# Down projection of a hybrid decoder step: the late loads move from GpSimd's queue to SyncE's, and four sums are added to the output later

## The chip, the cores and the metric

The kernel runs on one core of a Trainium2 chip. The metric is the device time of one execution in microseconds (us). The engines of the core are TensorE (PE: matmuls, and PEld for its weight loads), VectorE (DVE), ScalarE (ACT), GpSimd (POOL) and SyncE (SP), which here only issues DMAs and waits. They run their own programs side by side and meet at semaphores. DMAs that SP issues are in a hardware queue (q1 in the profile), those that POOL issues in a software queue (q0); both are served by the same 16 DMA engines.

## The reference

One inference step of a one-layer decoder with 1024 prompt tokens and 32 sample tokens: projection, sparse attention, a state-space mixer, and at the end the feed-forward part. The change touches only the last product of it:

```python
def finish(x, o_att, y_ssd, W):
    mix = jnp.concatenate([o_att..., y_ssd...], axis=-1)
    h = x + mix @ W['w_out']
    u = rmsnorm(h, W['norm_ffn'])
    return h + (jax.nn.silu(u @ W['w_gate']) * (u @ W['w_up'])) @ W['w_down']
```

All is float32; g = silu(u @ w_gate) * (u @ w_up) has 1056 rows (tokens) and 2816 columns, w_down is 2816 x 1024, the result is 1056 x 1024.

## The kernel before, in words

The stages run one after another: projection, prompt attention, state-space mixer, sample attention, output mixing, feed-forward. The last, `stage_ffn`, first makes g in 11 turns over pairs of column blocks (L2911 is its matmul), then does the down projection.

**The product.** The down projection is a fast 2 x 2 matrix multiplication with seven products instead of eight. Tokens are cut into two halves of 512 (32 tokens are left over), the 2816 inner rows into 11 pairs (`PAIRS`) of two 128-row blocks, the 1024 output columns into two halves of 512 (`NC`). `DOWN = (5, 3, 2, 4, 1, 6, 7)` is the order of the products. Each product takes 11 steps, one per pair, so there are 77 steps; step j belongs to group n = j // 11. A step needs a block of g sums (`g_x`, called gd_whole in the profile, 128 x 512, computed in the first part and stored in DRAM as g_sums) and one piece of w_down or the sum of two (`w`, `w_x`).

**float32 by parts.** g and w are each split into a high part, rounded for the matmul, and the low rest. ACT makes the high parts (gd_hi L3201, wd_hi L3196), DVE the sums of w (wd_whole, L3263) and the low parts (gd_lo L3275, wd_lo L3270). TensorE multiplies three combinations (L3244), each 128 rows x 512 columns. A step has four tiles q = 0 to 3 of 128 tokens, so 12 matmuls. In the groups of products 3 and 2 (n = 1 and 2) there are four more matmuls a step (L3254) for the 32 leftover tokens, called rest.

**Buffers.** g has six slots (`G_SLOTS`). SP loads the block of step j when step j - 6 has been used by PE (`s.used`), in `down_sync`. The w parts have ten slots.

**PSUM and drains.** A product gathers its 11 steps in four PSUM tiles, one for each q. Six banks are in turn (`D_BANKS`), so at a group's first step tiles 2 and 3 need the banks of tiles 0 and 1 of the group just before. PE waits for `s.drained` there. `drains(n)` in `down_vector` adds a finished product's tiles to y_sums in SBUF (L3293): two additions a tile for products 5, 3, 2, 4 and 1, one for 6 and 7. y_sums starts as h, which is loaded from DRAM; `drains(0)` waits for its top half (`h_in[0]`, four loads), `drains(1)` for the bottom half. DVE's program is one list: at step j it does the low part of w, that of g, the sum of w for the next step or the one after, and, at one place in each group, the drains of the group before. `D_ADDED_AT` gives that place.

**Loads.** SP loads the first pieces w(1,1) and the first g blocks while the last turn of the first part is still running. All else (rest, h, w(0,1), w(0,0), w(1,0), and the rest rows of h) is issued by POOL in `down_pool` at once, when the first part's matmuls are done and its last stores have landed. POOL has no other work by then.

Of the kernel before, what the change touches and what calls it, by code (L numbers as in the profile page):

```python
# [17 lines left out]
P = 128  # L18
# [15 lines left out]
NS = DB * DS  # L34
# [2625 lines left out]
NC = DM // 2  # L2660
PAIRS = FT // 2
# [3 lines left out]
D_W = {1: ((0, 0), (1, 1), ALU.add), 2: ((0, 0),), 3: ((0, 1), (1, 1), ALU.subtract), 4: ((1, 0), (0, 0), ALU.subtract), 5: ((1, 1),),  # L2665
       6: ((0, 0), (0, 1), ALU.add), 7: ((1, 0), (1, 1), ALU.add)}
D_REST = {3: ((0, 1), (1, 1)), 2: ((0, 0), (1, 0))}
D_ADDED_AT = {3: 2, 2: 3, 4: 3, 1: 3, 6: 3, 7: 3}
D_INTO = {1: ((0, 0, ALU.add), (1, 1, ALU.add)), 2: ((1, 0, ALU.add), (1, 1, ALU.subtract)), 3: ((0, 1, ALU.add), (1, 1, ALU.add)),
          4: ((0, 0, ALU.add), (1, 0, ALU.add)), 5: ((0, 0, ALU.subtract), (0, 1, ALU.add)), 6: ((1, 1, ALU.add),), 7: ((0, 0, ALU.add),)}  # L2670
D_BANKS, D_REST_BANKS = (6, 0, 7, 1, 3, 2), (4, 5)
# [7 lines left out]
def g_block(i, p):  # L2679
    return (i - 1) * PAIRS + p  # L2680
# [28 lines left out]
def stage_ffn(nc, io, m):  # L2709
# [5 lines left out]
    top = Region(nc, m.gate_raw_end, m.end)  # L2715
# [17 lines left out]
    d = place_down(nc, m, m.base_end + 14 * kh * QUARTER * 4, d_low, io)  # L2733
# [23 lines left out]
    with stage(nc, "landed*2 w_sum w_hi w_split u_sum u_sum_pool u_hi u_split m_done copied c_done silu_done g_ready "  # L2757
# [3 lines left out]
        with nc.Block() as block:  # L2761
            @block.sync
            def _(sp):
# [50 lines left out]
                load(slice(0, 1), 1)  # L2814
                over_pairs(sp, turn)
                down_sync(sp, s, d)

            @block.scalar
# [102 lines left out]
            @block.gpsimd  # L2921
            def _(pool):
                for k in range(POOL_SUMS):
                    i, a, b, op = U_SUMS[k]
                    nc.gpsimd.tensor_tensor(m.u_whole[1, i][:, :, :], m.u_whole[1, a][:, :, :], m.u_whole[1, b][:, :, :],
                                            op).then_inc(s.u_sum_pool, 1)
                down_pool(pool, s, d)

            @block.vector
            def _(dve):  # L2930
# [128 lines left out]
def place_down(nc, m, early_end, low_at, io):  # L3059

    early, late = Region(nc, m.base_end, early_end), Region(nc, early_end, m.end)
    g_x, g_lo, g_hi, w_x, w_lo, w_hi = [], [], [], [], [], []
    for name, slots, x, lo, hi in (("g", G_SLOTS, g_x, g_lo, g_hi), ("w", W_SLOTS, w_x, w_lo, w_hi)):
        for k in range(slots):
            region = early if k < D_EARLY else late
            x.append(nc.alloc_sbuf_tensor_at(f"{name}d_whole_{k}", [P, NC], F32, offset=region.at))
            lo.append(region(f"{name}d_lo_{k}", [P, NC], F32R))
            hi.append(region(f"{name}d_hi_{k}", [P, NC], F32R))
    w = {(1, 1): [early(f"w_22_{p}", [P, NC]) for p in range(PAIRS)]}
    w[0, 1] = [late(f"w_12_{p}", [P, NC]) for p in range(PAIRS)]  # L3070
    rest = late("rest_parts", [P, FT, 2 * NS], F32R)
    rest_x = late("rest_whole", [P, FT, NS])
    y = late("y_sums", [P, 2, 4, DM])
    for r in range(2):
        w[r, 0] = [late(f"w_{r + 1}1_{p}", [P, NC]) for p in range(PAIRS)]
    rest_y = late("rest_y", [P, DM])
    rest_low = nc.alloc_sbuf_tensor_at("rest_low", [P, NC], F32, offset=low_at)
    return named(g_x=g_x, g_lo=g_lo, g_hi=g_hi, w_x=w_x, w_lo=w_lo, w_hi=w_hi, w=w, rest=rest, rest_x=rest_x, y=y,
                 rest_y=rest_y, rest_low=rest_low, bank=m.bank, g_dram=m.g_dram, rest_dram=m.rest_dram, h_dram=io.h_dram,
                 wd=io.w_down.rearrange("o (f p) n -> p (o f) n", p=P), yp=io.y_prompt.rearrange("o n c -> (o n) c"),  # L3080
                 ys=io.y_sample.rearrange("b t c -> (b t) c"))


def rest_rows(k):

    return slice(2 * QUARTER * k + NC, 2 * QUARTER * (k + 1))


def w_number(piece, p):
    return (2 * piece[0] + piece[1]) * PAIRS + p  # L3090


def down_load_w(engine, s, d, piece, p):
    r, c = piece
    engine.dma_start(d.w[piece][p][:, :], d.wd[:, 2 * p + r, c * NC:(c + 1) * NC]).then_inc(s.w_in[w_number(piece, p)], 16)


def down_load_g(sp, s, d, j):
    i, p = DOWN[j // PAIRS], j % PAIRS
    sp.dma_start(d.g_x[j % G_SLOTS][:, :], d.g_dram[:, g_block(i, p), :]).then_inc(s.g_in[j % G_SLOTS], 16)  # L3100


def down_first_loads(sp, s, d):
    for j in range(D_EARLY):
        down_load_w(sp, s, d, (1, 1), j)
        down_load_g(sp, s, d, j)
    for p in range(D_EARLY, PAIRS):
        down_load_w(sp, s, d, (1, 1), p)
# [4 lines left out]
        down_load_g(sp, s, d, j)  # L3113


def down_pool(pool, s, d):
    top = [("h", 0, q) for q in range(4)]
    bottom = [("h", 1, q) for q in range(4)]
    w = lambda r, c, p: ("w", (r, c), p)
    later = ["rest"]  # L3120
    for q in range(4):
        later += [top[q], w(0, 1, q)]
    later += [w(0, 1, p) for p in range(4, PAIRS)] + bottom
    later += [w(r, 0, p) for p in range(PAIRS) for r in range(2)] + ["rest_h"]

    def one_of(what):
        if what == "rest":
            pool.wait_ge(s.plain_stored, 32 * PAIRS)
            pool.wait_ge(s.second_stored, 48 * PAIRS)
            pool.wait_ge(s.s5_stored, 16 * PAIRS)  # L3130
            pool.wait_ge(s.first_stored, 48 * PAIRS)
            pool.dma_start(d.rest_x[:, :, :], d.rest_dram[:, :, :]).then_inc(s.rest_in, 16)  # L3132
        elif what == "rest_h":
            for k in range(2):
                pool.dma_start(d.rest_y[k * NS // 2:(k + 1) * NS // 2, :], d.h_dram[rest_rows(k), :]).then_inc(s.rest_h_in, 16)
        elif what[0] == "h":
            r = 2 * QUARTER * what[1] + P * what[2]
            pool.dma_start(d.y[:, what[1], what[2], :], d.h_dram[r:r + P, :]).then_inc(s.h_in[what[1]], 16)
        else:
            down_load_w(pool, s, d, what[1], what[2])  # L3140

    pool.wait_ge(s.m_done, 28 * PAIRS)
    for what in later:
        one_of(what)


def down_sync(sp, s, d):
    def store(a, c, q):
        r, cols = 2 * QUARTER * a + P * q, slice(c * NC, (c + 1) * NC)
        inside = min(P, SEQ - r)  # L3150
        sp.dma_start(d.yp[r:r + inside, cols], d.y[0:inside, a, q, cols]).then_inc(s.y_stored, 16)
        if inside < P:
            sp.dma_start(d.ys[0:P - inside, cols], d.y[inside:P, a, q, cols]).then_inc(s.y_stored, 16)

    def stores(n, a, c):
        for q in range(4):
            sp.wait_ge(s.drained, DRAINED[4 * n + q])
            store(a, c, q)

    for j in range(G_SLOTS, D_STEPS):  # L3160
        sp.wait_ge(s.used, j - G_SLOTS + 1)
        if j == PAIRS - 1:
            sp.wait_ge(s.s5_stored, 16 * PAIRS)
        down_load_g(sp, s, d, j)
        if j == 31:
            stores(1, 0, 1)
        if j == 45:
            sp.wait_ge(s.rest_y, 2)
            sp.dma_start(d.yp[rest_rows(0), :], d.rest_y[0:NS // 2, :]).then_inc(s.y_stored, 16)
            sp.dma_start(d.ys[NS // 2:NS, :], d.rest_y[NS // 2:NS, :]).then_inc(s.y_stored, 16)  # L3170
        if j == 53:
            stores(3, 1, 0)
    stores(5, 1, 1)
    stores(6, 0, 0)
    sp.wait_ge(s.y_stored, 16 * 20)
# [103 lines left out]
def down_vector(nc, dve, s, d, last_token_sums):  # L3279
    def drains(n):  # L3280
        if n < 2:
            dve.wait_ge(s.h_in[n], 16 * 4)
        if n > 0:
            dve.wait_ge(s.drained, DRAINED[4 * n - 1])
        for q in range(4):
            if q < 3:
                dve.wait_ge(s.tile_done, 3 * n + q + 1)  # L3287
            else:
                dve.wait_ge(s.used, PAIRS * (n + 1))
            got = d.bank[D_BANKS[(4 * n + q) % len(D_BANKS)]][:, :]  # L3290
            for a, c, op in D_INTO[DOWN[n]]:
                y = d.y[:, a, q, c * NC:(c + 1) * NC]
                nc.vector.tensor_tensor(y, y, got, op).then_inc(s.drained, 1)  # L3293
# [15 lines left out]
    for j in range(2, D_STEPS):  # L3309
        if j == 4:  # L3310
            last_token_sums()
        if j == 9:
            dve.wait_ge(s.rest_hi, 1)
            nc.vector.tensor_tensor(d.rest[:, :, NS:2 * NS], d.rest_x[:, :, :], d.rest[:, :, 0:NS].bitcast(F32),
                                    ALU.subtract).then_inc(s.rest_split, 1)
        if j > PAIRS and j % PAIRS == D_ADDED_AT[DOWN[j // PAIRS]]:
            drains(j // PAIRS - 1)
# [151 lines left out]
```

## Time and profile before

| | before |
|---|---|
| median of 3 runs | 1769.87 us (1769.34 to 1775.06) |
| profiled execution | 1769.87 us, span 1768.1 us |
| busy: PE, PEld, DVE | 95%, 81%, 65% |
| busy: ACT, POOL | 43%, 24% |
| mean granted TensorE clock | 0.983 of full speed |
| DMA, SP's queue q1 | 121.66 MB |
| DMA, POOL's queue q0 | 80.46 MB |
| down projection, first to last PE start | 1533.7 to 1764.0 us |

The span goes from the first to the last instruction of the program; the time of an execution has a little around it. Busy time of PE is the time in which at least one matmul is under way; matmuls overlap, so a matmul of 0.39 us can start every 0.23 us. An idle time is shown in brackets before the instruction that ends it, with the one that released it. DMA landing times are counted from the issue. A time in the rows below is counted from the start of the span.

### The profile page before, as it was taken

What the parts mean: (1) busy time and instruction counts of PE and PEld (TensorE: products, weight loads), DVE (VectorE), ACT (ScalarE), POOL (GpSimd) and SP (SyncE); (2) the same over time, 40 slices, a digit from 0 to 9 for tenths busy, and PEclk for the clock granted to TensorE, in tenths of its full rate; (3) what the DMA queues carried; (4) which work ended last, traced back from release to release, by engine and by line L of the source; (5) the groups of instructions that cost most, each with busy time, mean ns of one, the idle gap of its engine ahead of it and who ended that gap; (6) DMA issues with size and microseconds to landing.
All of it is one profiled execution on the core that took longest, in us unless ns stands there. A gap on an engine that the chain in (4) does not pass through costs nothing. (4 is left out here: it accounts for less than half of the span.)

```text
span 1768.1 us, 32859 instructions
## 1 busy us (share of the span) xinstructions
PE 1673.0 (95%) x11957; PEld 1427.5 (81%) x11957; DVE 1151.3 (65%) x2521; ACT 764.2 (43%) x1593; POOL 431.9 (24%) x532
## 2 busy tenths in 40 slices
PE   5999999899998989998987996999999999999999
PEld 5999999688877666655655876999999999977887
DVE  6632247765665655556464368977777888687885
ACT  6322453677774235456443233433232233365342
POOL 1421110766664553334352001000000000050000
PEclk9999999899999999999998998999999999999999
DMA  5633211121001247547593232332222233493343
GB/s 157 105 104 107 53 43 26 25 50 24 21 15 25 67 127 283 196 136 273 175 396 135 72 98 63 100 104 90 93 93 90 95 108 102 160 390 97 95 119 107
DMA packets 158855, 204.19 MB, mean 115 GB/s; under 512 B 55110, under 2 KB 109423, under 8 KB 158674
## 3 DMA queue, kind: packets, MB, share of 16 engines
q1 hardware_dynamic: 136058, 121.66, 23.1%
q0 software_dynamic: 22368, 80.46, 12.9%
q8 instruction: 73, 1.20, 0.3%
q10 hardware_dynamic: 312, 0.52, 0.1%
q14 instruction: 44, 0.36, 0.1%
HBM read 164.69 MB, written 37.90 MB: 115 GB/s over the span
## 5 line engine op out<-in xcount | busy, mean ns | idle before, releaser
L2911 PE MATMUL banks<-u_sum,w_sum 128*128 128x264 f32 x3696 | 450.0, 284 | 9.7 <-DVE w_sum L2945 9.7
L2911 PEld LDWEIGHTS banks<-u_sum,w_sum 128*128 128x128 f32 x3696 | 449.7, 189 | 9.9 <-issue 9.8
L470 PE MATMUL banks<-u_parts_mix,w_in_parts 128*128 128x352 f32 x1440 | 244.2, 327 | 4.5 <-DVE u_parts_mix L837 4.5
L470 PEld LDWEIGHTS banks<-u_parts_mix,w_in_parts 128*128 128x128 f32 x1440 | 231.2, 189 | 7.8 <-DVE u_parts_mix L837 4.9
L1979 PE MATMUL banks<-turned,cmp_w 128*128 128x512 f32 x256 | 133.2, 603 | 4.7 <-DVE turned L2106 3.0
L2104 ACT ACTIVATE turned<-banks 128x512 f32<-128x512 f32 (+1 forms) x136 | 78.8, 587 | 125.0 <-PE banks L1967 124.8
L3244 PE MATMUL banks<-wd_hi,gd_hi 128*128 128x512 f32 x308 | 119.9, 389 | 1.0 <-DVE gd_lo L3275 1.0
L3244 PE MATMUL banks<-wd_lo,gd_hi 128*128 128x512 f32 x308 | 120.0, 390 | 0.0
L3244 PE MATMUL banks<-wd_hi,gd_lo 128*128 128x512 f32 x308 | 119.9, 389 | 0.0
L1967 PEld LDWEIGHTS banks<-consts,rows_grouped 128*128 128x128 f32 x512 | 64.7, 144 | 66.9 <-issue 57.1
L3132 POOL DMA_DIRECT2D rest_whole<-g_rest x1 | 0.6, 594 | 464.4 <-DMA g_sums<-silu_gate 464.4
L2834 ACT ACTIVATE w_sum<-w_whole 128x512 fp32r<-128x512 f32 x110 | 66.6, 624 | 105.9 <-DVE w_whole L2939 105.9
L1588 PE MATMUL banks<-key_parts,q_parts 128*128 128x512 f32 (+3 forms) x384 | 98.7, 367 | 12.6 <-POOL q_parts L1689 7.5
L2568 PE MATMUL banks<-w_out,mixT 128*128 128x512 f32 (+1 forms) x432 | 103.8, 398 | 0.8 <-DVE w_out L2602 0.8
L2568 PEld LDWEIGHTS banks<-w_out,mixT 128*128 128x128 f32 (+1 forms) x432 | 77.6, 182 | 23.4 <-DVE w_out L2602 1.9
L2106 DVE COPY turned<-banks 128x512 f32<-128x512 f32 x86 | 59.2, 691 | 52.2 <-PE banks L1967 51.1
L1588 PEld LDWEIGHTS banks<-key_parts,q_parts 128*128 128x128 f32 x384 | 64.0, 194 | 30.2 <-issue 14.2
L790 POOL TENSOR_TENSOR w_in_parts<-w_in_raw,w_in_parts 128x512 fp32r<-128x512 f32 (+1 forms) x39 | 54.5, 1417 | 135.0 <-ACT w_in_parts L621 134.9
L1967 PE MATMUL banks<-consts,rows_grouped 128*128 128x128 f32 x512 | 78.3, 278 | 8.3 <-DVE rows_grouped L2213 6.7
L1709 POOL TENSOR_SCALAR p_win_cmp<-p_win_cmp,row_scale,gates 128x640 f32<-128x640 f32 (+12 forms) x128 | 70.4, 565 | 57.0 <-DVE row_scale L1752 57.0
L2945 DVE TENSOR_TENSOR w_sum<-w_whole,w_sum 128x512 fp32r<-128x512 f32 x110 | 77.4, 707 | 5.4 <-ACT w_sum L2834 4.2
L3201 ACT ACTIVATE gd_hi<-gd_whole 128x512 fp32r<-128x512 f32 x77 | 48.1, 625 | 56.7 <-DMA gd_whole<-g_sums 56.2
(440 smaller groups left out, 3191.2 us busy)
## 6 DMA issues: line engine op xcount, KB each, us to landing
gd_whole<-g_sums SPq DMA_DIRECT2D x77, 256.0 KB, 2.7
g_sums<-silu_gate SPq DMA_DIRECT2D x55, 256.0 KB, 2.1
w_gate_raw<-in_w_gate SPq DMA_DIRECT2D x11, 1024.0 KB, 5.4
w_up_raw<-in_w_up SPq DMA_DIRECT2D x11, 1024.0 KB, 5.3
w<-in_w_down POOLq DMA_DIRECT2D x33, 256.0 KB, 18.9
w_in_raw<-in_w_in SPq DMA_DIRECT2D x29, 256.0 KB, 3.5
g_sums<-s SPq DMA_DIRECT2D x22, 256.0 KB, 2.3
x_tile<-in_x_prompt SPq DMA_DIRECT2D x8, 512.0 KB, 4.3
```

The lines of the kernel that those rows point to most:

```text
L470: mm = nc.tensor.matmul(bank[:, 0:PIECE], w[:, pb, :], u[:, pa, k, tokens(p)], start=(k == 0 and (pa, pb) == TERMS[0]), stop=(k == KT - 1 ...
L1588: mm = nc.tensor.matmul(out, qs[:, u % Q_UNITS, part, i % 2, :], k, start=part == HI, stop=part == LO)
L1709: x = nc.gpsimd.tensor_scalar(p, p, scale[:, u, r, br:br + 1], gate(r, br), ALU.mult, ALU.mult)
L1967: x = nc.tensor.transpose(m.bank[3 + f % 3][0:width, k * P:(k + 1) * P], src, c("ident"))
L1979: mm = nc.tensor.matmul(m.bank[u % 2][:, :], m.cmp.w1[:, u % 2, q, :, :].rearrange("p j h -> p (j h)"), w.fill[:, f % SLOTS, :], start=(q ...
L2104: x = nc.scalar.activation(to, src, ACT.Copy)
L2106: x = nc.vector.tensor_copy(to, src)
L2568: mm = nc.tensor.matmul(m.bank[2 * (j % 2) + h][0:r, :], mT[:, j % 2, a, k, 0:r], wo[:, b, k, h * 512:(h + 1) * 512], start=(k == 0 and (a ...
L2834: nc.scalar.activation(wp[side, p][:, HI, :, :], src, ACT.Copy).then_inc(s.w_hi, 1)
L2911: mm = nc.tensor.matmul(bank(tg, i), wp[side, p][:, a, k, :], m.u[tg, i, b][:, k, :], start=(k == 0 and (a, b) == TERMS[0]), stop=(k == kh ...
L2945: nc.vector.tensor_tensor(wp[side, p][:, LO, :, :], src, wp[side, p][:, HI, :, :].bitcast(F32), ALU.subtract).then_inc(s.w_split, 1)
L3244: mm = nc.tensor.matmul(d.bank[D_BANKS[tile % len(D_BANKS)]][:, :], g[a][:, q * P:(q + 1) * P], w[b][:, :], start=p == 0 and (a, b) == TER ...
```

## The change

There are two edits. The first changes `D_ADDED_AT`, the places of the drains in DVE's program: the drains of product 2 stand in the group of product 4 at place 4 instead of 3, those of products 4, 1 and 6 in the groups of products 1, 6 and 7 at place 5 instead of 3. The second removes `down_pool`. Its list of loads, in a slightly changed order (two w(0,1) pieces behind each h tile), goes to `down_sync` on SP, which issues two entries of the list after each g load from step 6 on. The waits for the stores of the first part that stood before the load of rest on POOL now stand on SP.

```diff
-D_ADDED_AT = {3: 2, 2: 3, 4: 3, 1: 3, 6: 3, 7: 3}
+D_ADDED_AT = {3: 2, 2: 3, 4: 4, 1: 5, 6: 5, 7: 5}
...
-                down_pool(pool, s, d)
...
-def down_pool(pool, s, d):
+def down_sync(sp, s, d):
...
     for q in range(4):
-        later += [top[q], w(0, 1, q)]
-    later += [w(0, 1, p) for p in range(4, PAIRS)] + bottom
+        later += [top[q], w(0, 1, 2 * q), w(0, 1, 2 * q + 1)]
+    later += [w(0, 1, p) for p in range(8, PAIRS)] + bottom
     later += [w(r, 0, p) for p in range(PAIRS) for r in range(2)] + ["rest_h"]
...
         if what == "rest":
-            pool.wait_ge(s.plain_stored, 32 * PAIRS)
+            sp.wait_ge(s.plain_stored, 32 * PAIRS)
...
-    pool.wait_ge(s.m_done, 28 * PAIRS)
-    for what in later:
-        one_of(what)
...
         down_load_g(sp, s, d, j)
+        for what in later[:2]:
+            one_of(what)
+        later = later[2:]
```

SP's program behind the last stores of g sums, before. gd_whole is a g block, the number its slot; the first row here is step 6.

```order
L2773 DMA g_sums<-silu_gate 128x512 x2
L3100 DMA gd_whole_14293<-g_sums 128x512
L3100 DMA gd_whole_14296<-g_sums 128x512
L3100 DMA gd_whole_14299<-g_sums 128x512
L3100 DMA gd_whole_14302<-g_sums 128x512
L3100 DMA gd_whole_14305<-g_sums 128x512
```

The same place in the changed kernel:

```order
L2773 DMA g_sums<-silu_gate 128x512 x2
L3099 DMA gd_whole_14293<-g_sums 128x512
L3131 DMA rest_whole<-g_rest 128x704
L3137 DMA y_sums<-h_dram 128x1024
L3099 DMA gd_whole_14296<-g_sums 128x512
L3094 DMA w_0_14352<-in_w_down 128x512
L3094 DMA w_1_14353<-in_w_down 128x512
L3099 DMA gd_whole_14299<-g_sums 128x512
L3137 DMA y_sums<-h_dram 128x1024
L3094 DMA w_2_14354<-in_w_down 128x512
L3099 DMA gd_whole_14302<-g_sums 128x512
```

The loads of rest (behind the waits for the stores), of h and of w now stand between the g loads of steps 6, 7, 8 and 9. In this manner it goes on to step 27. Up to the g load of step 12 there are the rest, four h tiles and seven w pieces ahead of it.

DVE's program before, at the place where the drains of product 4 (y_sums) stand in the group of product 1: the first row is the low part of g for step 46, and the second the w sum for step 48.

```order
L3275 TENSOR_TENSOR gd_lo_14306<-gd_whole_14305,gd_hi_14307 128x512
L3263 TENSOR_TENSOR wd_whole_14314<-w_4_14370,w_4_14345 128x512
L3293 TENSOR_TENSOR y_sums<-y_sums,banks 128x512 x8
L3270 TENSOR_TENSOR wd_lo_14312<-wd_whole_14311,wd_hi_14313 128x512
L3275 TENSOR_TENSOR gd_lo_14309<-gd_whole_14308,gd_hi_14310 128x512
L3263 TENSOR_TENSOR wd_whole_14317<-w_5_14371,w_5_14346 128x512
```

The same place in the changed kernel:

```order
L3271 TENSOR_TENSOR gd_lo_14306<-gd_whole_14305,gd_hi_14307 128x512
L3259 TENSOR_TENSOR wd_whole_14314<-w_4_14370,w_4_14345 128x512
L3266 TENSOR_TENSOR wd_lo_14312<-wd_whole_14311,wd_hi_14313 128x512
L3271 TENSOR_TENSOR gd_lo_14309<-gd_whole_14308,gd_hi_14310 128x512
L3259 TENSOR_TENSOR wd_whole_14317<-w_5_14371,w_5_14346 128x512
L3266 TENSOR_TENSOR wd_lo_14315<-wd_whole_14314,wd_hi_14316 128x512
L3271 TENSOR_TENSOR gd_lo_14294<-gd_whole_14293,gd_hi_14295 128x512
L3259 TENSOR_TENSOR wd_whole_14320<-w_6_14372,w_6_14347 128x512
L3289 TENSOR_TENSOR y_sums<-y_sums,banks 128x512 x8
```

The eight drains have moved back behind six instructions, the work of steps 47 and 48. The same holds in the groups of products 6 and 7; in the group of product 4 they move behind the work of one step.

## Rows read from the trace of the kernel before

**Rows 1.** The chain of waits, by line (shares of the span)
```profile
PE banks L2911 25%; PE banks L3244 12%; PE banks L3254 1%; DVE w_whole L2939 0%; DVE w_sum L2945 0%; DVE y_sums L3293 0%; DVE one_less_two L2976 0%; DVE gd_lo L3275 0%; DVE wd_lo L3270 0%; DVE silu_gate L2981 0%; ACT two L2840 0%; DVE one_less_five L2976 0%; DVE c L2976 0%; DVE one_less_five L3051 0%; DVEq L3287 0%
```
**Rows 2.** Timeline, PE (start us, length, engine, line, out<-in, [idle before <-releaser])
```profile
1533.66 0.47 PE L3244 MATMUL banks<-wd_hi,gd_hi 128*128 128x512 f32 x1 [1.03 <-DVE gd_lo L3275]
...
1565.03 0.39 PE L3244 MATMUL banks<-wd_hi,gd_hi 128*128 128x512 f32 x1
...
1567.31 0.40 PE L3244 MATMUL banks<-wd_hi,gd_hi 128*128 128x512 f32 x1
```
**Rows 3.** Timeline, ACT: high parts of g for steps 46, 48, 59, 70
```profile
1669.10 0.63 ACT L3201 ACTIVATE gd_hi<-gd_whole 128x512 fp32r<-128x512 f32 x1 [1.38 <-DMA gd_whole<-g_sums]
...
1674.64 0.63 ACT L3201 ACTIVATE gd_hi<-gd_whole 128x512 fp32r<-128x512 f32 x1 [1.59 <-DMA gd_whole<-g_sums]
...
1704.41 0.63 ACT L3201 ACTIVATE gd_hi<-gd_whole 128x512 fp32r<-128x512 f32 x1 [1.38 <-DMA gd_whole<-g_sums]
...
1734.46 0.63 ACT L3201 ACTIVATE gd_hi<-gd_whole 128x512 fp32r<-128x512 f32 x1 [1.65 <-DMA gd_whole<-g_sums]
```
**Rows 4.** Timeline, DVE: low parts of g, and drains
```profile
1532.82 0.69 DVE L3275 TENSOR_TENSOR gd_lo<-gd_whole,gd_hi 128x512 fp32r<-128x512 f32 x1
...
1560.50 0.68 DVE L3275 TENSOR_TENSOR gd_lo<-gd_whole,gd_hi 128x512 fp32r<-128x512 f32 x1
...
1562.91 4.86 DVE L3293 TENSOR_TENSOR y_sums<-y_sums,banks 128x512 f32<-128x512 f32 x8
...
1669.76 0.69 DVE L3275 TENSOR_TENSOR gd_lo<-gd_whole,gd_hi 128x512 fp32r<-128x512 f32 x1 [0.64 <-ACT gd_hi L3201]
...
1672.67 4.87 DVE L3293 TENSOR_TENSOR y_sums<-y_sums,banks 128x512 f32<-128x512 f32 x8 [1.61 <-PE banks L3244]
```
**Rows 5.** Timeline, PE: first matmul of tile 2 in steps 44, 55, 66
```profile
1675.80 0.39 PE L3244 MATMUL banks<-wd_hi,gd_hi 128*128 128x512 f32 x1
...
1705.72 0.39 PE L3244 MATMUL banks<-wd_hi,gd_hi 128*128 128x512 f32 x1
...
1735.64 0.39 PE L3244 MATMUL banks<-wd_hi,gd_hi 128*128 128x512 f32 x1
```
**Rows 6.** Timeline, POOL: the first of its loads
```profile
1546.26 0.59 POOL L3132 DMA_DIRECT2D rest_whole<-g_rest  x1 [464.38 <-DMA g_sums<-silu_gate]
```
**Rows 7.** Timeline, SP's queue: seven issues in a row
```profile
1527.22 3.64 SPq L3095 DMA_DIRECT2D w<-in_w_down  x7
```
**Rows 8.** Instructions of the tile gd_whole, windows 1550 to 1560, 1600 to 1620
```profile
DMA to landing us min/median/max: 6.0/6.3/7.0
...
DMA to landing us min/median/max: 2.6/2.7/3.1
```
**Rows 9.** DMA issues: engine, operation, count, KB each, median us to landing
```profile
w<-in_w_down POOLq DMA_DIRECT2D x33, 256.0 KB, 18.9
...
y_sums<-h_dram POOLq DMA_DIRECT2D x8, 512.0 KB, 12.5
```
**Rows 10.** Windows: stretch, PE busy (starts), clock, DMA share, GB/s
```profile
1528.00:1538.00 10.00, 8.96 (x58) 1.00 1.03 370
1542.00:1548.00 6.00, 6.00 (x28) 1.00 1.00 349
1554.00:1586.00 32.00, 32.00 (x142) 1.00 1.03 414
1593.00:1613.00 20.00, 20.00 (x88) 1.00 0.26 69
```
**Rows 11.** Timeline and windows, PE: idle times and the clock after them
```profile
758.39 0.91 PE L1979 MATMUL banks<-turned,cmp_w 128*128 128x512 f32 x1 [2.78 <-DVE turned L2106]
...
758.70:762.10 3.40, 3.40 (x8) 0.51 0.00 0
...
924.46 1.06 PE L1967 MATMUL banks<-consts,scores_s 128*128 128x128 f32 x8 [2.31 <-ACT scores_s L2174]
...
924.50:935.00 10.50, 10.50 (x200) 1.00 0.54 183
```

More of the change, by code:

```diff
@@ L3090, in w_number, with down_load_w @@
     return (2 * piece[0] + piece[1]) * PAIRS + p
-def down_load_w(engine, s, d, piece, p):
+def down_load_w(sp, s, d, piece, p):
     r, c = piece
-    engine.dma_start(d.w[piece][p][:, :], d.wd[:, 2 * p + r, c * NC:(c + 1) * NC]).then_inc(s.w_in[w_number(piece, p)], 16)
+    sp.dma_start(d.w[piece][p][:, :], d.wd[:, 2 * p + r, c * NC:(c + 1) * NC]).then_inc(s.w_in[w_number(piece, p)], 16)
 def down_load_g(sp, s, d, j):
@@ L3127, in one_of @@
         if what == "rest":
-            pool.wait_ge(s.plain_stored, 32 * PAIRS)
[L3129 to L3132, printed above, removed]
+            sp.wait_ge(s.plain_stored, 32 * PAIRS)
+            sp.wait_ge(s.second_stored, 48 * PAIRS)
+            sp.wait_ge(s.s5_stored, 16 * PAIRS)
+            sp.wait_ge(s.first_stored, 48 * PAIRS)
+            sp.dma_start(d.rest_x[:, :, :], d.rest_dram[:, :, :]).then_inc(s.rest_in, 16)
         elif what == "rest_h":
             for k in range(2):
-                pool.dma_start(d.rest_y[k * NS // 2:(k + 1) * NS // 2, :], d.h_dram[rest_rows(k), :]).then_inc(s.rest_h_in, 16)
+                sp.dma_start(d.rest_y[k * NS // 2:(k + 1) * NS // 2, :], d.h_dram[rest_rows(k), :]).then_inc(s.rest_h_in, 16)
         elif what[0] == "h":
             r = 2 * QUARTER * what[1] + P * what[2]
-            pool.dma_start(d.y[:, what[1], what[2], :], d.h_dram[r:r + P, :]).then_inc(s.h_in[what[1]], 16)
+            sp.dma_start(d.y[:, what[1], what[2], :], d.h_dram[r:r + P, :]).then_inc(s.h_in[what[1]], 16)
         else:
-            down_load_w(pool, s, d, what[1], what[2])
-    pool.wait_ge(s.m_done, 28 * PAIRS)
-    for what in later:
-        one_of(what)
-def down_sync(sp, s, d):
+            down_load_w(sp, s, d, what[1], what[2])
     def store(a, c, q):
```

## The prediction

> **What bounds the kernel now.** I read the chain of waits first. TensorE stands in it alone over the last third: the down projection (L3244 with L3254) is the piece that the change touches, and between its first and last matmul the chain stays on PE [rows 1]. PE's timeline next: its only idle time in the stage is 1.03 us as it begins, a wait for gd_lo [rows 2]. From there 142 matmuls start in 32 us, and as many per us in a quiet stretch [rows 10]: 0.227 us apart, so a tile of three takes 0.68 and a step of four tiles 2.72 us. The third tile of step 11 starts at 1565.03 (so the step at 1563.67), and step 12 at 1567.31: 2.28 later, of which 1.36 are two tiles and about 0.93 the four matmuls (L3254) for the 32 leftover tokens [rows 2]. No wait is left that the change could take away. Every wait it adds on PE's path lengthens the run one for one.
>
> I count steps as the code does (j = 0 to 76), groups as n = j // 11, and "tile q" for the four PSUM tiles of a step. PE's rule is the key: in the first step of group n, tile 2 waits for the drain of tile 0 of group n-1, and tile 3 for that of tile 1 (six banks for four tiles a group). The drains are additions on DVE, placed in its program by D_ADDED_AT.
>
> **Part one: drains later on DVE.** Groups 1 and 2 keep their places. For the group with product 4 (n = 3) the drains go from j = 36 to 37, for n = 4, 5, 6 from place 3 to place 5, j = 49, 60 and 71. Nothing is added or removed, six DVE instructions now stand ahead of the drains. What they wait for decides. DVE cannot do gd_lo of step 48 before its g block is loaded, and that load waits until step 42 is done (six g buffers). ACT's gd_hi rows show this lockstep: 1669.10, 1674.64, each ended by the g load [rows 3]; they are steps 46 and 48. From gd_hi to gd_lo is 0.66 us (1669.10 to 1669.76), and DVE's pace is 0.60 us an instruction (8 drains in 4.87) [rows 3, 4]. So in n = 4:
> gd_lo of step 48 at 1674.64 + 0.66 = 1675.30; it and the sum for step 50 take 1.20, and the drains start at D = 1676.50 (before: 1672.67 [rows 4]).
> Tile 0 has two additions: drained at D + 0.60 + 0.69 = D + 1.29. Tile 1: D + 2.49.
> PE wakes 0.15 us after a DVE end, and its first matmul takes 0.08 more than the others (1532.82 + 0.69 = 1533.51 against 1533.66; 0.47 against 0.39) [rows 2, 4]. Tile 2 starts at D + 1.44, tile 3 at D + 2.64, and the next step at D + 2.64 + 0.08 + 0.68 = D + 3.40 = 1679.90. Before, tile 2 started at 1675.80 and the next step 1.36 later, 1677.16 [rows 5]. Loss: 2.7 us.
> n = 5: gd_hi 1704.41, D = 1704.41 + 1.86 = 1706.27, next step 1709.67 against 1705.72 + 1.36 = 1707.08: 2.6 us [rows 3, 5].
> n = 6: one addition a tile (product 6). gd_hi 1734.46, D = 1736.32, tile 2 at D + 0.69 + 0.15 = 1737.16, plus 0.08 is 1737.24 against 1735.64; tile 1 is drained in time. Loss 1.6 us [rows 3, 5].
> n = 3: its PE steps before are the long ones (about 3.65 us), so the same reckoning puts the drains about where tile 0 is finished anyway: cost 0. Cover: about 2 us of slack before step 33 needs them.
> Sum of part one: 6.9 us. Bounds: 0 if DVE were to have these g blocks early, which the gd_hi rows exclude; 8 if every link is 0.1 us longer. What is late next, after the drains, is gd_lo of the following step, which PE wants five steps on: free.
>
> **Part two: 44 loads from POOL to SP.** Removed: POOL's queue of 44 DMAs (one of rest, 8 of h, 33 of w, 2 of rest_h), starting at 1546.26, when the last g stores had landed [rows 6]. Added on SP: the same transfers, two after each g load from j = 6. SP's issue costs about 0.52 us (7 in 3.64) [rows 7]; three a step fit in 2.72. Queued behind the new waits are the g loads: SP stops after g(6) until 1546.26, then rest, h, g(7), w, w, g(8) and so on. In one queue a 256 KB g load waits for all bytes ahead of it; before, the g loads had their own queue, and landed in 6.0 to 7.0 us in the thick of POOL's traffic, 2.6 to 3.1 alone [rows 8].
> Price: up to g(12) there are rest (128 x 704 words, 0.36 MB), four h tiles (2.10 MB), six g blocks (128 x 512 words, as w has) and seven w (3.41 MB) [rows 9]. Rates: SP's burst of 256 KB blocks moved 370 GB/s, POOL's phase 414 [rows 10]. For h and rest I take 414, for the others 370: 5.9 + 9.2 = 15.1 us. A lone g load lands in 2.6 us of which 0.7 is data, so 1.9 fixed: g(12) lands at 1546.26 + 1.9 + 15.1 = 1563.3. The same sum gives g(7) at 1551.0, g(9) 1555.8, g(11) 1560.6: each 0.2 to 0.9 us ahead of what PE wants. But group 1's drains come on DVE behind gd_lo(12), and there gd_lo, then 2.41 us (1560.50 to 1562.91), then the drains [rows 4]. New D = 1563.3 + 0.1 + 0.66 + 2.41 = 1566.5, and step 12 starts at D + 3.40 + 0.93 = 1570.8 against 1567.31 [rows 2]: 3.5 us lost. Bounds: 0, if g(12) still lands within the 6 us of before; 6, if the queue moves 349 GB/s throughout, the lowest row [rows 10] (16.8 us of data, D 1.7 later), and g(7) or g(11), with 0.2 us to spare, hold PE up on their own. I take 3.5, since 370 is the row of just such a queue.
> The DMA page of the Trainium skill (DMA: Bandwidth & Descriptors, "Queues, rings and completion order") says that an engine takes turns between its queues packet by packet, while one queue's ring is consumed in order. By the first half the small g loads used to pass POOL's bulk (6 us against a median of 18.9 for w [rows 9]); by the second they now stand behind it. The trace agrees with the first; the second no row shows yet.
> The same page ("Specifications") puts HBM for one core at about 358 GB/s. Had that ruled here, g(12) would land 1.3 us later and part two would cost 4.8. The trace shows 414 for 32 us [rows 10], so the measurement decides.
> From step 12 on PE takes about 3.65 a step and SP brings 0.79 MB for it (215 GB/s): the backlog melts. Loads w(0,0), w(1,0) and h bottom are five steps ahead of use. POOL's absence gives nothing: it made nobody wait. Cover for all this is SP's idle time; nothing else waits on SP until the y stores.
>
> **Sum.** 6.9 + 3.5 = 10.4. The profiled execution took 1769.87 us (span 1768.1), which is also the median of the runs before. Forecast 1780.3.
>
> **Rivals.**
> A, queue harmless: the hardware queue delivers g(12) in time, only part one counts: 1769.9 + 6.9 = 1776.8. For: before, no g load took over 7.0 us even at 414 GB/s [rows 8]. Against: 5.9 MB must pass in 17 us, in one line.
> B, the clock: PE stood 2.78 us before 758.39 and then ran 3.4 us at 0.51, the 1.2 GHz level; after 2.31 us of idle before 924.46 it kept 1.00 [rows 11]. At step 11 my idle time is D + 1.44 = 1567.9 less 1565.19, where the last matmul ends, 2.7 us, at the others 2.0 and less. A fall costs half of 3.4 us, 1.7 us: one makes 1782.0, three 1785.4.
> C, drains harmless: DVE stands further ahead than I think, only the queue counts: 1773.4; or neither, 1770. Against: gd_hi rows.
> D, faster: POOL's bulk traffic slows the matmuls' reads, and their 0.227 us would fall to 0.213 (512 columns at 2.4 GHz) without it: 1012 matmuls x 0.0134 = 13.6 us, less 10.4 makes 1766.7. It decides as soon as the gain exceeds the 10.4 us of waits. Against it: 142 starts in 32 us at 414 GB/s and 88 in 20 us at 69 GB/s are one pace [rows 10].
>
> **How the numbers follow.** Forecast 0.50 (own range 1778.5 to 1781.3), A 0.17, B 0.18, C 0.13 (0.06 for 1773.4, 0.07 for about 1770), D 0.02. A measurement here tells 0.3% (5.3 us) from no change. Slower by more: forecast, A and B, 0.85. Within: C, 0.13. Faster: 0.02. The range leaves out most of C and the far end of B: 1774.8 to 1785.5.
>
> **What would show it.** In the changed profile PE should have idle time before L3240's matmuls, ended by DVE y_sums, at four places: 2 to 2.7 us at step 11 and 2, 1.9 and 1.4 at steps 44, 55 and 66, with short second ones of about 0.4 us in the first three. None at step 33. DVE's gd_hi wait before step 12 should rise, g loads around 1550 to 1560 take 7 us and more, and POOL have nothing to do. If PE waits there for gd_lo instead, my slack for g(7) to g(11) was too small. If there is no idle before the last three, the g lockstep was read wrongly, and if the clock shows a step below 1.00 behind one of them, it is B.

## The result and the profile after

The changed kernel is slower: 1787.83 us (median of 6 runs, 1785.83 to 1788.24) against 1773.45 us for the kernel before (6 runs, 1769.34 to 1775.06), a ratio of 1.0084 (95% interval 1.0073 to 1.0096), or 14.4 us. Forecast was 1780.3 (1774.8 to 1785.5), slower. The direction was right, and PE waits at all the places that were named, and at one more. The size was not right: 14.4 us instead of 10.4, and a time above the range.

| | before | after |
|---|---|---|
| profiled execution, span | 1769.87, 1768.1 us | 1803.71, 1801.9 us |
| first matmul of step 0 | 1533.66 | 1551.81 |
| first matmul of step 76 | 1761.48 | 1794.77 |
| stretch between the two | 227.82 us | 242.96 us |

The profiled execution of the changed kernel is 15.9 us longer than its own median, and more than half of what it has over the one before (18.15 of 33.84 us) comes ahead of the change. The first and last matmuls of the down projection stand in PE's timelines as follows; the first block is the kernel before, the second the changed one. The new_v row is among the last of the sample attention.

```profile
945.48 0.64 PE L2066 MATMUL banks<-new_v,turned 4*32 4x128 f32 x16
...
1761.48 0.39 PE L3244 MATMUL banks<-wd_hi,gd_hi 128*128 128x512 f32 x1
```

```profile
962.98 0.64 PE L2066 MATMUL banks<-new_v,turned 4*32 4x128 f32 x16
...
1551.81 0.47 PE L3240 MATMUL banks<-wd_hi,gd_hi 128*128 128x512 f32 x1 [1.03 <-DVE gd_lo L3271]
...
1794.77 0.39 PE L3240 MATMUL banks<-wd_hi,gd_hi 128*128 128x512 f32 x1
```

17.5 us of the 18.15 by which the stage begins late have arisen before the sample attention ends, in code that is the same. From the last new_v matmul to step 0 all 14 profiles of this document take 587 to 589 us. What the change does is in the stretch: 15.14 us more. That number, read from the same two matmuls of each profile, is the measure of all experiments below.

Where the stretch grew is seen in PE's idle times, which answer to [rows 2] and [rows 5] (the rows are of steps 7, 11, 44, 44, 55, 55, 66):

```profile
1572.09 0.47 PE L3240 MATMUL banks<-wd_hi,gd_hi 128*128 128x512 f32 x1 [1.00 <-DVE gd_lo L3271]
...
1586.98 0.79 PE L3240 MATMUL banks<-wd_hi,gd_hi 128*128 128x512 f32 x1 [2.40 <-DVE y_sums L3289]
...
1701.20 0.50 PE L3240 MATMUL banks<-wd_hi,gd_hi 128*128 128x512 f32 x1 [1.81 <-DVE y_sums L3289]
1702.40 0.58 PE L3240 MATMUL banks<-wd_hi,gd_hi 128*128 128x512 f32 x1 [0.23 <-DVE y_sums L3289]
...
1735.21 0.50 PE L3240 MATMUL banks<-wd_hi,gd_hi 128*128 128x512 f32 x1 [1.69 <-DVE y_sums L3289]
1736.40 0.50 PE L3240 MATMUL banks<-wd_hi,gd_hi 128*128 128x512 f32 x1 [0.23 <-DVE y_sums L3289]
...
1768.75 0.50 PE L3240 MATMUL banks<-wd_hi,gd_hi 128*128 128x512 f32 x1 [1.23 <-DVE y_sums L3289]
```

All four waits for the drains (y_sums) are where they were forecast, and step 33 has none. Not in the forecast's sum are the wait for gd_lo at step 7, and what two matmul lengths after the waits point to: 0.79 and 0.58 instead of 0.50. The windows tell why; columns as in [rows 10]:

```profile
1563.00:1566.00 3.00, 3.00 (x15) 1.00 0.71 214
1566.00:1572.00 6.00, 5.10 (x23) 1.00 0.92 311
1575.00:1584.00 9.00, 9.00 (x42) 1.00 1.05 409
1586.60:1590.00 3.40, 3.02 (x7) 0.50 1.04 419
1702.70:1706.10 3.40, 3.40 (x9) 0.50 0.26 77
1736.80:1740.20 3.40, 3.40 (x10) 0.50 0.27 77
1768.70:1772.10 3.40, 3.35 (x14) 1.00 0.15 26
```

Three times the granted clock falls to 0.50, the 1.2 GHz level, for 3.4 us as such a wait ends, and not at the last. At step 11 the fall (from 1586.6) begins 0.4 us before the wait is over, at steps 44 and 55 0.3 to 0.4 us behind the second, short wait. The first two rows show the other surprise: once SP could start its loads, 214 and then 311 GB/s were moved, and 409 only from 1575 on.

### The profile page after: what moved, and what is told of

It is laid out like the page before. It is cut to its first block and busy times, and to the rows that moved or that the text cites. A ratio compares the mean times of both kernels' runs of the same rounds, so it can differ in the third digit from the quotient of the medians.

```text
span 1801.9 us, 32859 instructions
## 1 busy us (share of the span) xinstructions
PE 1693.7 (94%) x11957; PEld 1436.6 (80%) x11957; DVE 1153.6 (64%) x2521; ACT 762.5 (42%) x1593; POOL 407.9 (23%) x488
## 5 line engine op out<-in xcount | busy, mean ns | idle before, releaser
L3240 PEld LDWEIGHTS banks<-wd_hi,gd_hi 128*128 128x128 f32 x308 | 58.9, 191 | 26.6 <-DVE y_sums L3289 10.4
```

The source lines that it names most:

```text
L3240: mm = nc.tensor.matmul(d.bank[D_BANKS[tile % len(D_BANKS)]][:, :], g[a][:, q * P:(q + 1) * P], w[b][:, :], start=p == 0 and (a, b) == TER ...
```

## Experiments

Each stretch is from the first matmul of step 0 to that of step 76; "loss" is what a step takes more than in the first profile of the kernel before, with what runs over into the step behind it. Steps are counted from first matmul to first matmul, so PE's wait before step 7 is a loss of step 6. The experiments were made in four groups (e1 to e4, e5 to e8, e9 and e10, e11 and e12), each on another chip; the medians of the kernel before in them were 1791.78, 1773.11, 1773.29 and 1773.59 us. So ratios are against the kernel before in the same group.

| run | stretch | losses by step | clock falls | ratio (interval) |
|---|---|---|---|---|
| changed (first profile) | 242.96 | 6: 1.2, 11: 4.1, 44: 4.2, 55: 4.1, 66: 1.5 | 3 | 1.0084 (1.0073 to 1.0096) |
| e1 drains only | 236.90 | 11: 0.5, 44: 2.7, 55: 4.2, 66: 1.5 | 1 | 1.0058 (1.0036 to 1.008) |
| e2 queue only | 232.36 | 6: 0.5, 11: 4.0 | 1 | 1.0019 (1.0004 to 1.0033) |
| e3 place four | 233.66 | 6: 1.3, 11: 4.5 | 1 | 1.0023 (1.0009 to 1.0036) |
| e4 changed again | 241.86 | 6: 1.1, 11: 2.9, 44: 4.2, 55: 4.2, 66: 1.5 | 2 | 1.0075 (1.0055 to 1.0094) |
| e5 light queue | 228.68 | 11: 0.8 | 0 | 1.0006 (0.9996 to 1.0016) |
| e6 place six | 248.88 | 44: 6.7, 55: 7.2, 66: 7.1 | 3 | 1.0121 (1.0104 to 1.0138) |
| e7 drains, seven slots | 227.88 | none | 0 | 0.9998 (0.9987 to 1.0008) |
| e8 changed, seven slots | 231.84 | 11: 3.9 | 1 | 1.0025 (1.0013 to 1.0038) |
| e9 before the sum | 233.46 | 11: 0.7, 44: 2.1, 55: 2.0, 66: 0.9 | 0 | 1.0023 (1.0013 to 1.0032) |
| e10 rest later | 231.87 | 11: 4.1 | 1 | 1.0022 (1.0012 to 1.0032) |
| e11 both cured | 228.39 | 11: 0.5 | 0 | 1.0001 (0.9992 to 1.001) |
| e12 before again | 228.45 | 11: 0.5 | 0 | one run |

**e1: the drains alone.** The kernel before with one line changed:

```diff
-D_ADDED_AT = {3: 2, 2: 3, 4: 3, 1: 3, 6: 3, 7: 3}
+D_ADDED_AT = {3: 2, 2: 3, 4: 4, 1: 5, 6: 5, 7: 5}
```

> The new drain places with POOL's loads as before. Theory: the two edits cost independently, each by waits of PE. The late places cost 4.2 us at step 44 and 4.1 at step 55 (2.7 and 2.6 by the wait for y_sums, the rest by a fall of the clock to 0.5 behind it) and 1.6 at step 66 (no fall), so the down projection's PE stretch (first to last matmul start, 227.8 us before and 243.0 in the changed kernel) becomes 237.7, 9.9 over before, and steps 6 and 11 cost nothing. Rival: the long waits at steps 44 and 55 need the loads on SP's queue (g loads delayed by them); then this kernel stays within 2 us of before.

Measured 236.9, with one fall of the clock where two were expected. The long waits need no queue on SP. At step 44 the clock did not fall here, and the loss is the bare wait, 2.74 us; at 55 it fell, and the loss is 4.2. PE's timeline at step 44, and the clock in windows behind steps 44 and 55:

```profile
1700.13 0.50 PE L3244 MATMUL banks<-wd_hi,gd_hi 128*128 128x512 f32 x1 [1.93 <-DVE y_sums L3293]
1701.33 0.51 PE L3244 MATMUL banks<-wd_hi,gd_hi 128*128 128x512 f32 x1 [0.23 <-DVE y_sums L3293]
```

```profile
1700.50:1704.00 3.50, 3.27 (x15) 1.00 0.17 36
1734.00:1737.40 3.40, 3.40 (x9) 0.52 0.22 67
```

In 3.4 us at half clock 9 matmuls start instead of 15: about 1.4 us lost. At step 44 the changed kernel, with a fall, loses 4.2 us and e1, without one, 2.74: 1.5 us is the price of a fall behind this wait.

**e2: the queue alone.** The changed kernel with the old table:

```diff
-D_ADDED_AT = {3: 2, 2: 3, 4: 4, 1: 5, 6: 5, 7: 5}
+D_ADDED_AT = {3: 2, 2: 3, 4: 3, 1: 3, 6: 3, 7: 3}
```

> The loads on SP's queue with the old drain places. Theory: PE waits 1.2 us for gd_lo of step 7 and loses 4.1 at step 11 (drains behind a late gd_lo of step 12, and a clock fall), nothing at steps 33, 44, 55, 66: stretch 233.1 us, 5.3 over before. Rival: the loss of the changed kernel comes from the drains alone, and the queue is harmless: 228 us.

Measured 232.36: losses at steps 6 and 11 alone, at step 6 with 0.5 us less than half of what was expected (1.2). The excesses of e1 and e2 over 227.82 (9.1 and 4.5) make 13.6, the changed kernel's two profiles have 14.0 (e4) and 15.1; the ratios add up likewise (0.58 + 0.19 = 0.77% against 0.75% in the same group, each known to 0.1 to 0.2). So the costs of the edits add up. e1 and e2 have two falls of the clock together, as e4 has, and the first profile has three.

**e3: place 4 instead of 5.** The changed kernel with

```diff
-D_ADDED_AT = {3: 2, 2: 3, 4: 4, 1: 5, 6: 5, 7: 5}
+D_ADDED_AT = {3: 2, 2: 3, 4: 4, 1: 4, 6: 4, 7: 4}
```

> The loads on SP's queue, and the drains of products 4, 1, 6 at place 4 instead of 5. Theory (DVE in lockstep with the g loads, one step of 2.72 us for each place): the drains begin 1.1 us later than at place 3, at 1673.8 on the clock of the kernel before, tile 0 is drained 0.6 us and tile 1 0.1 us before PE wants them, so no wait at steps 44, 55, 66, stretch as with the queue alone, 233.1 us (up to 0.5 more). Rival: the loss grows evenly with the place, so place 4 costs about half of the 9.9 us: 238.

233.66, no loss at 44, 55 and 66. One place decides between nothing and 2.7 us. (1.3 us more than e2 come from steps 6 and 11 to 12, before any of these places.)

**e6: place 6.** The kernel before with

```diff
-D_ADDED_AT = {3: 2, 2: 3, 4: 3, 1: 3, 6: 3, 7: 3}
+D_ADDED_AT = {3: 2, 2: 3, 4: 3, 1: 6, 6: 6, 7: 6}
```

> POOL's loads as before, drains of product 2 at the old place 3 for product 4, those of 4, 1 and 6 at place 6. Theory (DVE in lockstep with g loads, 2.72 us a place): each loss is 2.7 us above that of place 5: 5.5 at step 44, 5.3 at 55, 4.3 at 66, and since PE now stands 3.8 us and more in one piece the clock falls behind all three, 1.5 us each: stretch 227.8 + 15.1 + 4.5 = 247.4 (243 without falls). Rival: drains wait for PE, not for g loads, so that one place more costs only the 1.8 us of DVE's three instructions: about 241.

248.88. The wait at step 44:

```profile
1684.37 0.50 PE L3244 MATMUL banks<-wd_hi,gd_hi 128*128 128x512 f32 x1 [4.44 <-DVE y_sums L3293]
```

4.44 against 1.93 in e1: 2.5 us more for one place, nearer to a PE step (2.72) than to DVE's 1.8. The clock fell at all three, at 55 and 66 for 6.8 us, and there the fall began 1.7 and 0.8 us before PE's wait was over. So these two losses are larger than expected (7.2 and 7.1 against 6.8 and 5.8).

**e7: drains alone, with seven g slots.** On top of e1:

```diff
-G_SLOTS, W_SLOTS, D_EARLY = 6, 10, 4
+G_SLOTS, W_SLOTS, D_EARLY = 7, 10, 4
...
-    rest_x = late("rest_whole", [P, FT, NS])
+    rest_x = early("rest_whole", [P, FT, NS])
```

> The new drain places (4, 5, 5, 5) and POOL's loads, with seven g slots instead of six (rest_whole moved to another place in SBUF to make room). Theory: the seventh slot puts each g load a step earlier, so gd_lo of step 48 is done 2.7 us earlier and place 5 becomes as cheap as place 4 was with six slots: no wait at steps 44, 55, 66, stretch 227.8 to 228.3 us. Rival: DVE's own work ahead of the drains is what is late; then the slot changes nothing: 236.9, as with the drains alone.

227.88: nothing is lost. DVE's timeline has the same instructions ahead of the drains as the changed kernel, only earlier against PE:

```profile
1676.27 0.69 DVE L3275 TENSOR_TENSOR gd_lo<-gd_whole,gd_hi 128x512 fp32r<-128x512 f32 x1 [0.82 <-ACT gd_hi L3201]
1676.88 0.68 DVE L3263 TENSOR_TENSOR wd_whole<-w,w 128x512 f32<-128x512 f32 x1
1677.48 4.87 DVE L3293 TENSOR_TENSOR y_sums<-y_sums,banks 128x512 f32<-128x512 f32 x8
```

This profile's stage starts 3.67 us later (1537.33), so the drains start at 1673.81 on the clock of before, just what was worked out for one step less of lockstep (1673.8).

**e9: the drains one instruction earlier.** e1 with the drains of the last three groups ahead of the w sum:

```diff
-        if j > PAIRS and j % PAIRS == D_ADDED_AT[DOWN[j // PAIRS]]:
+        if j > PAIRS and j // PAIRS < 4 and j % PAIRS == D_ADDED_AT[DOWN[j // PAIRS]]:
...
+        if j // PAIRS >= 4 and j % PAIRS == D_ADDED_AT[DOWN[j // PAIRS]] - 1:
+            drains(j // PAIRS - 1)
         ahead = j + (1 if DOWN[j // PAIRS] == 3 else 2)
```

> POOL's loads, and in the groups of products 1, 6 and 7 the drains one DVE instruction earlier than at place 5: behind gd_lo of step 48 (59, 70), ahead of the w sum that followed it. Theory of the waits: each loss shrinks by that sum's 0.6 us: waits of about 1.4 and 0.4 us at steps 44 and 55 and 0.8 at 66, losses 2.1, 2.1 and 1.0. Theory of the clock (a fall needs a wait of about 1.9 us or more): no fall in this stage; stretch 227.8 + 5.2 = 233.0. Rival: falls come with any broken pace, then they appear behind steps 44 and 55 here too, 1.5 us each: 236.

233.46, losses 2.1, 2.0 and 0.9, no fall. The rival, by which any broken pace brings one, did not show in this profile. Each wait shrank by 0.6 to 0.7 us, about the sum's 0.6, and at step 55 the price of e1's fall is gone too. PE's idle time at step 44 was then:

```profile
1682.31 0.50 PE L3244 MATMUL banks<-wd_hi,gd_hi 128*128 128x512 f32 x1 [1.23 <-DVE y_sums L3293]
1683.51 0.51 PE L3244 MATMUL banks<-wd_hi,gd_hi 128*128 128x512 f32 x1 [0.23 <-DVE y_sums L3293]
```

**e5: a lighter queue.** The changed kernel with the old table, and in `down_sync`

```diff
-    later = ["rest"]
-    for q in range(4):
-        later += [top[q], w(0, 1, 2 * q), w(0, 1, 2 * q + 1)]
-    later += [w(0, 1, p) for p in range(8, PAIRS)] + bottom
+    later = [top[0], top[1], "rest", w(0, 1, 0), w(0, 1, 1), top[2], top[3]]
+    later += [w(0, 1, p) for p in range(2, PAIRS)] + bottom
...
-        for what in later[:2]:
+        count = {6: 1, 7: 1, 8: 2, 9: 2, 10: 1, 11: 1, 12: 2}.get(j, 3)
+        for what in later[:count]:
...
```

> All loads on SP's queue, old drain places, but in another order and at another pace: h tiles first (one each behind g(6), g(7)), rest with its wait for the stores only behind g(8), only three w pieces up to g(12), and from step 13 on three loads a step until the list is done. Theory: the queue costs through its bytes ahead of g(7) and g(12) (1.15 and 5.9 MB behind a wait until the stores landed). Now 4.8 MB stand ahead of g(12) and they start 3 us earlier, so g(12) lands before 1560 on the clock of before, and no wait is left at steps 6 and 11: stretch 227.8 to 228.5 us, and the time is that of the kernel before. Rival: SP's hardware queue is too slow for these loads in any order (about 340 GB/s as it starts), then 2 to 4 us stay.

228.68, time as before (1.0006). The queue on SP can carry these loads for nothing; the stretch is 0.2 us above what was expected, and of the 0.8 us at step 11 e12 shows that 0.5 occur in the kernel before too. The edit changes several things at once (the order, the pace, and where the wait for the stores stands), so it shows that they cure together, not which of them does.

**e10: rest moved back, with the wait for the stores.** The changed kernel with the old table and

```diff
     later += [w(r, 0, p) for p in range(PAIRS) for r in range(2)] + ["rest_h"]
+    later = later[1:5] + [later[5], "rest"] + later[6:]
```

> All loads on SP's queue two a step, old drain places, with one entry moved: rest with its wait for the stores stands as sixth of the list (behind g(8)), not as first. The bytes ahead of g(12) are those of the changed kernel (5.9 MB), but they start 2.6 us earlier, since nothing waits for the stores in between. Theory: no wait at step 6, and at step 11 the loss shrinks by these 2.6 us, from 2.9 to 4.0 with the queue alone to about 0.5 to 1.3, without a fall of the clock: stretch 228.3 to 229.1. Rival: the bytes alone decide (the queue is the bound from the start); then step 11 still loses 3 to 4 us, and the stretch is 231 to 232.

231.87: the number is the rival's, but the trace shows another cause. Step 6 is cured, so its loss came from the wait for the stores that stood ahead of g(7). Step 11 still loses 4.1 with a fall of the clock; its wait is 1.71 us.

```profile
1572.12 0.50 PE L3241 MATMUL banks<-wd_hi,gd_hi 128*128 128x512 f32 x1 [1.71 <-DVE y_sums L3290]
```

What made DVE late here is the load that was moved. ACT waits for rest, and DVE for ACT's part of it:

```profile
1560.12 0.79 ACT L3213 ACTIVATE rest_parts<-rest_whole 128x704 fp32r<-128x704 f32 x1 [1.77 <-DMA rest_whole<-g_rest]
```

```profile
1560.95 0.89 DVE L3311 TENSOR_TENSOR rest_parts<-rest_whole,rest_parts 128x704 fp32r<-128x704 f32 x1 [1.87 <-ACT rest_parts L3213]
...
1568.38 0.68 DVE L3272 TENSOR_TENSOR gd_lo<-gd_whole,gd_hi 128x512 fp32r<-128x512 f32 x1
...
1570.79 0.68 DVE L3290 TENSOR_TENSOR y_sums<-y_sums,banks 128x512 f32<-128x512 f32 x1
```

From rest_parts to the drains DVE has 16 instructions and no idle time; the low part of g(12), at 1568.38, waits for nothing. So the bytes ahead of g(12) are not what this run lost its time to, and it does not decide between the two theories.

**e8: the changed kernel with seven slots** (the edit of e7).

> The changed kernel with seven g slots. Theory: late losses gone as above. SP's list now starts behind g(7), so step 6 loses nothing, and 4.8 MB instead of 5.9 stand ahead of g(12): drains begin about 1564.3 on the clock of before instead of 1567, loss 1 to 1.5 us at step 11, no fall of the clock: stretch 229 us. Rival: step 11's loss does not depend on the bytes ahead of g(12): it stays at 3 to 4, 231 to 232.

231.84. Late losses and step 6's are gone as expected. Step 11 still lost 3.9 with a fall, against 1 to 1.5 expected, though 4.8 MB stand ahead of g(12) as in e5, which lost 0.8. DVE's timeline there has no idle time from the low part of g for step 11 to the drains at 1569.01:

```profile
1564.19 0.69 DVE L3271 TENSOR_TENSOR gd_lo<-gd_whole,gd_hi 128x512 fp32r<-128x512 f32 x1 [0.70 <-ACT gd_hi L3197]
...
1569.01 2.47 DVE L3289 TENSOR_TENSOR y_sums<-y_sums,banks 128x512 f32<-128x512 f32 x4
```

That is eight instructions at 0.60 us behind a late g(11). I had counted only the bytes ahead of g(12). DVE's own pace behind any late input is the second bound at this place.

**e11: both cures in one kernel**: e5's list (shifted by the one step that the seventh slot brings), the new places, seven slots.

> All loads on SP's queue in the light order (h tiles first, rest behind the third g load of the list, three w pieces up to the drains), the new drain places, and seven g slots. Theory: both causes are gone, since each cure has shown itself alone (0.9 us left with the light order, 0.1 with seven slots): stretch 227.8 to 228.7 us, time that of the kernel before within 0.1%, no better, because TensorE has no wait left to give. Rival: the cures need each other's slack (late drains with a queue on SP), then 2 us or more stay.

228.39, ratio 1.0001: both causes are gone, and nothing is won.

**e4 and e12: the two kernels once more.**

> The changed kernel once more, unchanged. Theory: the 18 us by which its profiled execution was behind the kernel before when the down projection began come from the gathers of the sample attention in that one execution, not from the change; here the stretch is again 243 us (within 1), the clock falls again behind steps 11, 44 and 55, not behind 66, and the start of the stretch lies within 6 us of 1533.7. Rival: the edit shifts something ahead of the down projection too; then the start is late by 18 us again.

> The kernel before once more, for a second profile. Theory: the stretch from first to last step is 227.8 us as in the first profile (up to 0.7 more by a short wait at step 11, as two kernels with POOL's loads showed), while the start of the stretch scatters by some us because the sample attention's gathers do. Rival: the first profile of the kernel before was a lucky one and its stretch is 2 us or more longer here, which would take that much off the change's loss.

e4: 241.86, but the clock fell only behind 44 and 55. Step 11 lost 2.9 there, 4.1 in the first profile. The start of the stretch, 1553.64, was late again, beyond the 6 us expected; e1 in the same group starts at 1555.31 and e2 at 1556.79, and there the kernel before itself took 1791.78 us. The later groups' profiles, of kernels with and without the change's parts, start at 1535.5 to 1538.9. So the late start goes with the group of runs (its chip or its time, which these runs do not separate), and in the first profile with that one execution, and not with the edit. e12: 228.45, with a wait of 0.23 us before a matmul at step 11 that the first profile did not have. The changed kernel's loss in the stretch is 13.4 to 15.1 us.

## Why the prediction was wrong in size

**Bound, and the place of the waits: right.** PE had nothing to gain, and every new wait lengthened the run.

**Part one, drains (forecast 6.9 us, measured 9.8): mechanism right, one term missing.** The bare losses came out: at step 44 in e1 it is 2.74 (forecast 2.7), at step 66 it is 1.5 (1.6). n = 3 cost 0. e3, e6 and e7 show the lockstep with the g loads from three sides. In the first profile steps 44 and 55 lost 4.2 and 4.1 because the clock fell behind both, 1.5 each. Two losses of 2.7 and 2.6 with these falls, and 1.5, make the 9.8.

**The step that failed: the sum put the fall of the clock at nothing.** It stood only in rival B, with a chance of 0.18. I set the danger at 2.7 us and took 2.0 and less as safe, because one idle time of 2.31 us had been followed by a clock of 1.00 [rows 11]. In the changed kernel falls came with idle times of 2.40 us, and of 1.81 and 1.69 us that had a second one of 0.23 behind them. In e1 none followed 1.93 and 0.23, in e9 none 1.23 and 0.23. One row at which a thing does not happen is no bound. What the falls cost can be told with the prediction's own rule, by which the next step starts at D + 3.40, and 0.93 later where the rest matmuls stand. D, the start of the drains, was at steps 11, 44 and 55:

```profile
1585.65 0.68 DVE L3289 TENSOR_TENSOR y_sums<-y_sums,banks 128x512 f32<-128x512 f32 x1
...
1699.87 4.86 DVE L3289 TENSOR_TENSOR y_sums<-y_sums,banks 128x512 f32<-128x512 f32 x8
...
1733.87 2.48 DVE L3289 TENSOR_TENSOR y_sums<-y_sums,banks 128x512 f32<-128x512 f32 x4
```

The rule gives bare losses of 3.3, 2.7 and 2.6 us; measured are 4.1, 4.2 and 4.1. In e4, where the clock did not fall at step 11, the rule gives 2.9 and measured is 2.9. So the three falls cost 0.8, 1.5 and 1.5 us, 3.8 in all. At step 11 a fall costs less, since it began before PE's wait was over. B's own three falls made 15.5 us over before (1785.4), and the stretch has 15.1. That they are so near is in part luck: B had 1.7 us for each fall and nothing for step 6. Given the waits, B was the likely case and not one in six.

**Part two, queue (forecast 3.5 us, measured 5.3): mechanism right, two terms wrong.** The bare loss at step 11, 3.3 us, is near the 3.5 of the forecast; the fall's 0.8 us are in the term above. The other missing term is step 6, which was put at nothing and lost 1.25 us (0.5 in e2): g(7) had no slack of 0.2 us. ACT's gd_hi for step 7 started here, after 5.00 us of waiting,

```profile
1570.59 0.63 ACT L3197 ACTIVATE gd_hi<-gd_whole 128x512 fp32r<-128x512 f32 x1 [5.00 <-DMA gd_whole<-g_sums]
```

that is 1552.44 on the clock of before; with 1551.0 for the landing and 0.1 for the wake it was forecast for 1551.1. I had put h and rest at 414 GB/s, the mean of a phase long under way [rows 10], but the phase begins slowly. It did so in the kernel before too, with the loads in POOL's queue:

```profile
1546.00:1549.00 3.00, 3.00 (x15) 1.00 0.95 327
1549.00:1552.00 3.00, 3.00 (x15) 1.00 0.90 334
1552.00:1555.00 3.00, 3.00 (x15) 1.00 0.99 369
1555.00:1558.00 3.00, 3.00 (x15) 1.00 1.03 412
```

So the slow first 9 us are not a property of SP's queue. New in the changed kernel are the 214 GB/s of its first 3 us, after SP had stood still from 1561.76 to 1563.72 for the stores. SP's rows from there on show one slow issue (1.31 us for the first h tile):

```profile
1563.72 0.34 SPq L3131 DMA_DIRECT2D rest_whole<-g_rest  x1
1564.11 1.31 SPq L3137 DMA_DIRECT2D y_sums<-h_dram  x1
1565.47 0.43 SPq L3099 DMA_DIRECT2D gd_whole<-g_sums  x1
```

By g(12) this was partly made good: gd_hi for step 12 started at 1582.57, or 1564.4, against 1563.4 forecast. It sets the drains only just: DVE has no idle time above 0.05 us from the low part of g(10) on, so g(10), g(11) and g(12) allow the same start within 0.1 us. The landing times answer to [rows 8]; first the window 1563 to 1576 of the changed kernel, then 1570 to 1580 of the kernel before:

```profile
DMA to landing us min/median/max: 5.1/7.5/9.1
```

```profile
DMA to landing us min/median/max: 5.9/6.4/7.3
```

The second row also corrects rival A in the prediction, which had no g load over 7.0 us. The Trainium skill's rule (DMA: Bandwidth & Descriptors, "Queues, rings and completion order") that one queue's ring is taken in order agrees with this: behind bulk in their own queue g loads take up to 9.1 us, beside bulk in another 7.3 at most. The 358 GB/s of the same page of the Trainium skill ("Specifications") were no ceiling here either: 409 GB/s from 1575 to 1584. But from 1564 to 1582 the mean was 341 GB/s, below the 349 that the forecast had as its lowest bound. What in the queue costs the 3.3 us at step 11 (the bytes ahead of g(12), the wait for the stores, the place of rest) is not separated by these runs: e5 changes all three, and in e10 and e8 other inputs of DVE were the late ones.

**The reference point.** The forecast was set against 1769.87 us. With the three runs made beside the changed kernel, the kernel before has a median of 1773.45, 3.6 us more. The range reached 15.6 us above its own reference, and the change's 14.4 us lie within that. The time fell out of the range because this and the 4.0 us missing in the sum came together; either alone would have left it inside.

**A, C and D** fell: the queue was not harmless in this order (e2), the drains neither (e1), and POOL's silence did not speed up the matmuls: all steps of the changed kernel outside its losses take what they took before within 0.1 us, where D had PE 0.16 us faster a step.

## What to carry to other kernels

Where one engine works in lockstep with a ring of buffers, moving its work back in program order by one ring step is free until it touches the deadline, and from there costs whole steps of the bound engine. Count from the last input that comes late, and add the engine's own instructions behind it (16 of them in e10, eight in e8). A transfer that must arrive soon does not belong behind bulk in the same queue: order a queue by first need and spread it, and price its start by its slow beginning. When an experiment gives a rival's number, read in the trace whether it is the rival's cause; in e10 it was not. And a wait of about 2 us on TensorE should be priced with the clock fall that may come with it, here 1.5 us on top of 2.7.

## What the runs showed of the hardware

The granted clock fell to 0.50 for 3.4 us (6.8 at two waits in e6) with waits of 1.69 to 4.56 us, but not always. At step 11 it fell with waits of 1.70 and 1.71 us (e8, e10) and not with 2.07 (e4), and the same wait at step 44 (1.8 to 1.9 us with a second of 0.23) was followed by a fall in two profiles and by none in a third. Taken with the short second wait, PE stood 1.9 us or more 15 times in these stages, and 13 times the clock fell; it stood 1.2 to 1.5 us five times (e9, and step 66), and it never fell. Nothing between was measured. The fall began between 1.7 us before and 0.8 us behind the end of the wait. The profiles do not tell what decides, and it stays open. Matmuls that start after a wait for the drains take 0.50 us instead of 0.39 even with the clock at 1.00. With the late loads in POOL's queue the core moved 327 to 369 GB/s in their first 9 us and 412 after that, with them in SP's queue 214 to 350 GB/s in the first 11 us and 409 after that; why they begin slowly is not shown. And the part before the stage, the same program, took up to 23 us more in one profile than in another (step 0 at 1533.7 to 1556.8), with the late ones in the group of e1 to e4 and in the changed kernel's first profile. What is slower there was not looked into.
